# Two model blocks in one kernel: score banks claimed pair by pair, Fourier pieces by halves of the sequence, the first turning and one weight rounding issued earlier

## The reference

```python
for l in range(DEPTH):
    h = _rms_norm(x, norm_g[l])
    p = h @ w_in[l]
    c_q, c_kv, k_pe, z_a, u_f, z_f, g_a, g_f = _split_in(p)
    o_a = _mla_branch(c_q, c_kv, k_pe, ...)                # 8 heads, 96 = 64 + 32 (rotated) dimensions
    y_a = (o_a * jax.nn.silu(z_a)) @ w_attn_proj[l]
    y_f = (_fourier_branch(u_f) * jax.nn.silu(z_f)) @ w_fourier_proj[l]
    m = (jax.nn.sigmoid(g_a + b_merge[l, 0]) * y_a
         + jax.nn.sigmoid(g_f + b_merge[l, 1]) * y_f)
    x = x + m @ w_out[l]
```

## Time and profile before

| what | value |
|---|---|
| time, median of 3 runs | 2191.68 us (2191.34 to 2194.15) |
| profiled execution, its time | 2191.92 us |
| profiled execution, its span | 2190.1 us |
| granted TensorE clock, mean | 0.995 of full speed |
| busy: TensorE, VectorE, ScalarE, GpSimd | 97%, 43%, 42%, 35% of the span |
| instructions | 29154 |

### The profile page before, as it was taken

How to read it: one execution, slowest core, us unless ns; L and a number is a source line. 1 busy time by engine, 2 the same in 40 slices (tenths; PEclk the granted TensorE clock), 3 DMA queues, 4 the chain that set the end, 5 groups by cost and what they waited for, 6 DMA issues and landing times.

```text
span 2190.1 us, 29154 instructions
## 1 busy us (share of the span) xinstructions
PE 2126.9 (97%) x11190; PEld 1660.1 (76%) x11190; DVE 949.3 (43%) x1470; ACT 927.8 (42%) x1442; POOL 759.4 (35%) x316
## 2 busy tenths in 40 slices
PE   6999999999999998999999999999899999989999
PEld 5677778888888885667888888777578887856887
DVE  7674462111126267775211112654633354454331
ACT  5642264233245324774422324554643244555231
POOL 3332134444443630003444444334034443401443
PEclk9999999999999999999999999999999999999999
DMA  4232122232332420002333233222013332201332
GB/s 150 68 100 77 53 80 93 91 100 93 96 97 91 134 83 20 1 1 81 97 97 96 96 97 97 77 87 86 1 58 96 97 96 87 78 20 39 97 97 87
DMA packets 60166, 174.84 MB, mean 80 GB/s; under 512 B 17040, under 2 KB 17168, under 8 KB 60048
## 3 DMA queue, kind: packets, MB, share of 16 engines
q1 hardware_dynamic: 47456, 168.38, 24.4%
q10 hardware_dynamic: 12592, 4.75, 0.9%
HBM read 169.44 MB, written 3.67 MB: 79 GB/s over the span
## 4 chain that ended last, share of the span: by engine, by line
issue 65%; POOL 21%; PE 12%; ACT 1%; POOLq 1%; DVE 0%; DVEq 0%
POOL w_lo L2549 21%; PE banks L731 4%; PE banks L733 3%; PE banks L732 3%; PE banks L1235 1%; ACT prob L1808 1%; ACT probT L1815 0%; PE banks L1247 0%; PE banks L1239 0%; ACT prob_far L1808 0%; POOLq L2553 0%; POOLq L2555 0%; PE banks L1213 0%; PE banks L1291 0%; POOLq L2549 0%
## 5 line engine op out<-in xcount | busy, mean ns | idle before, releaser
L2549 POOL TENSOR_TENSOR w_lo<-raw,w_hi 128x1024 fp32r<-128x1024 f32 x312 | 759.2, 2435 | 1414.5 <-ACT w_hi L1375 1414.4
L731 PE MATMUL banks<-h_lo,w_hi 128*128 128x512 f32 x1408 | 570.5, 405 | 23.1 <-DVE h_lo L1910 12.2
L733 PE MATMUL banks<-h_hi,w_hi 128*128 128x512 f32 x1408 | 554.3, 394 | 0.0
L732 PE MATMUL banks<-h_hi,w_lo 128*128 128x512 f32 x1408 | 550.3, 391 | 0.0
L1375 ACT ACTIVATE w_hi<-raw 128x1024 fp32r<-128x1024 f32 x312 | 328.1, 1053 | 509.0 <-PE banks L733 497.6
L731 PEld LDWEIGHTS banks<-h_lo,w_hi 128*128 128x128 f32 x1408 | 266.1, 189 | 89.0 <-POOL w_lo L2549 16.4
L732 PEld LDWEIGHTS banks<-h_hi,w_lo 128*128 128x128 f32 x1408 | 265.9, 189 | 60.6 <-issue 4.4
L733 PEld LDWEIGHTS banks<-h_hi,w_hi 128*128 128x128 f32 x1408 | 265.7, 189 | 60.8
L731 PE MATMUL banks<-a_lo,w_hi 128*128 128x512 f32 x768 | 304.3, 396 | 0.0
L733 PE MATMUL banks<-a_hi,w_hi 128*128 128x512 f32 x768 | 301.5, 393 | 0.0
L732 PE MATMUL banks<-a_hi,w_lo 128*128 128x512 f32 x768 | 298.7, 389 | 0.0
(11 more groups left out here) (360 smaller groups left out, 2513.7 us busy)
## 6 DMA issues: line engine op xcount, KB each, us to landing
raw<-in_weights SPq DMA_DIRECT2D x312, 512.0 KB, 3.5
x<-in_x SPq DMA_DIRECT2D x4, 512.0 KB, 6.7
out<-x SPq DMA_DIRECT2D x8, 256.0 KB, 2.0
phase<-in_phase ACTq DMA_DIRECT2D x1, 706.0 KB, 4.1
phase<-in_phase ACTq DMA_DIRECT2D x1, 704.0 KB, 4.0
ld_dram<-Ld ACTq DMA_DIRECT2D x1, 512.0 KB, 5.0
Ls<-ld_dram ACTq DMA_DIRECT2D x1, 512.0 KB, 4.8
inv_dram<-inv ACTq DMA_DIRECT2D x1, 512.0 KB, 2.8
```

The source lines that it names most:

```text
L731: mm(out, w_hi, x_lo, start=first, stop=False)
L732: mm(out, w_lo, x_hi, start=False, stop=False)
L733: return mm(out, w_hi, x_hi, start=False, stop=last)
L2549: return nc.gpsimd.tensor_tensor(c.w_lo[:, slot, :], c.raw[:, slot, :], c.w_hi[:, slot, :].bitcast(F32), ALU.subtract)
```

## The change

It has four parts, all in the second block, and each is made in both layers.

1. `scores` claims the bank pair of its first item, issues that item's two 64-row matmuls, and then claims the second pair.
2. The transposes of item 0 are issued before the scores of quad 1, and no longer behind them.
3. The Fourier pieces are made half by half (`k` outside, `g` inside) on all engines. The Fourier products wait only for the pieces of their own half, go group by group within a half, and the first three groups announce themselves singly.
4. ScalarE rounds the block two beyond that of the values before the exponentials of the key roots, by `passed("v2", l, 0)`.

```diff
@@ -462,10 +462,10 @@
         for n in range(len(MLA_ITEMS)):
             take_pair(("s2", l, n), (2, 4)[n % 2])
             take_pair(("t2", l, n), 6)
-        for g in range(FG):
-            for k in range(FK):
+        for k in range(FK):
+            for g in range(FG):
                 scratch("dd", l, g, k)
-        gemm([("f", l, g) for g in range(FG)], FK)
+        gemm([("f", l, g) for g in range(FG)], FK, apart=True)
         splits(*[("of", l, g) for g in range(FG)])
         for m in range(KT):
             each("ga", l, m, n=1)
@@ -1229,8 +1229,9 @@
         def scores(quad):
             jj, qt = quad // NT, quad % NT
             t, keys = slice(qt * P, qt * P + P), [("s2", l, 2 * quad + i) for i in range(2)]
-            outs = [claim_pair(key) for key in keys]
+            outs = []
             for i in range(2):
+                outs.append(claim_pair(keys[i]))
                 for s in range(2):
                     mm(outs[i][:, s, :], c.q2[pair[s], 4 + 2 * jj + i, t], c.k2[pair[s], 2 * jj + i, :], start=True, stop=False)
             for i in range(2):
@@ -1271,10 +1272,11 @@
             gemm((("za", "zf")[z // 4], l, z % 4), h_hi, h_lo)
             if z in (1, 2):
                 query_sums(2 * z, 2 * z + 2)
+        turned_probs(0)
         for q in range(1, MLA_QUADS + 2):
             if q < MLA_QUADS:
                 scores(q)
-            if q <= MLA_QUADS:
+            if 1 < q <= MLA_QUADS:
                 turned_probs(2 * q - 2)
             if q > 1:
                 values(2 * q - 3)
@@ -1296,17 +1298,17 @@
                 ins.then_inc(fill(key), 1)
         outs = [claim(("f", l, g)) for g in range(FG)]
         first = block[("f", l, 0)][0]
-        for g in range(FG):
-            for k in range(FK):
-                read(("dd", l, g, k))
         for k in range(FK):
             pe.wait_ge(c.w_lo_ready, first + k + 1)
-            for part in range(2):
-                w, d = slice(part * T, part * T + T), slice(part * P, part * P + P)
-                for g in range(FG):
-                    slot = (first + k) % RING
+            slot, last = (first + k) % RING, k == FK - 1
+            for g in range(FG):
+                read(("dd", l, g, k))
+                for part in range(2):
+                    w, d = slice(part * T, part * T + T), slice(part * P, part * P + P)
                     ins = three(outs[g][:, :], c.d_hi[:, k, g, d], c.d_lo[:, k, g, d], c.w_hi[:, slot, w], c.w_lo[:, slot, w],
-                                k == part == 0, k == FK - 1 and part == 1)
+                                k == part == 0, last and part == 1)
+                if last and g < FG - 1:
+                    ins.then_inc(fill(("f", l, g)), 1)
             ins.then_inc(c.block_used, 1)
         for m in range(KT):
             gemm(("ga", l, m, 0), h_hi, h_lo)
@@ -1779,6 +1781,7 @@
 
         value_out(0)
         value_out(1)
+        passed("v2", l, 0)
         for i in range(4):
             read(("hs2", l, "k", i))
             f(c.k_root[:, i, :], c.k_root[:, i, :], ACT.Exp, scale=-0.5).then_inc(c.k_root_ready, 1)
```

## The result

The changed kernel takes 2181.16 us (median of 5 runs, 2179.26 to 2182.59); the kernel before took 2191.75 beside it. The ratio is 0.9945, 95% interval 0.993 to 0.9959. The forecast was 2174.8 us, in a range of 2170.5 to 2179: it had the direction and missed the size. Of 16.9 us forecast, 10.6 came.

What follows compares the result with a forecast made beforehand. TensorE was taken as the bound, so gains lay in its waits. Per layer 5.1 - 0.56 + 1.2 + 1.1 + 1.6 = 8.44 us, 16.9 for two, gave 2174.8 us; range 2170.5 to 2179.

Steps and rivals of the forecast that it cites:

- the end of the Fourier products: Before the first merge gate: signalling groups singly removes TensorE's 0.88 us wait and the slow start, 1.1 us saved a layer.
- some later stage gives the time back: Listed sign of being wrong: time saved is lost again later in the kernel; given no size or chance.
- The split claim: Attention's quad loop: half the first pair's scores run inside the wait; 0.85 us saved a quad, 5.1 us a layer.
- the 7.5 that I had named as a sign of being wrong: Quad loop: period forecast at about 7.6 us; above 8 or under 7.5 us would show the forecast wrong.
- the row that I went by: Second pair's weight load: starts only at the wait's end, giving 0.85 us a quad; loading ahead would give 0.93.
- the 0.26 us from ScalarE's read to the scores: Quad loop: delay from ScalarE's last read of a bank pair to scores, used to place the first pair's claim at 1546.06.
- The price of 0.08 us for the late start: Scores' second half: passes beginning after a wait are slower at first, about 0.08 us added to its 0.98 us.
- The first turning: Item 0's transposes ahead of the second quad's scores: exponentials and the next claim come later, 0.56 us lost a layer.
- The rounding: Second attention gate's weight block rounded before the key roots: TensorE's 1.41 us wait and slow start go, 1.6 us saved.
- The pieces: Fourier pieces made half by half: first product starts behind the last piece without its 1.13 us wait, 1.2 us saved.
- that rival: A Fourier wait comes back, from late banks or GpSimd's roundings: 2.3 us of a layer lost, 2179.4 us; chance 8%.
- The loop's last wait: Before the last quad's transposes: the 1.84 us wait stays, since it hangs on ScalarE's four exponentials.

## Why the prediction missed

**The step that failed** is the one on the end of the Fourier products: "The wait of 0.88 goes, and with it the slow start [...] I take 1.1 us, bounds 0.88 and 1.15." The wait and the slow start did go (1.0 us). What was left out is that the wait also separated two rows of matmuls with different paces. Without it the 767 matmuls behind keep the Fourier products' 233.3 ns, 4.4 ns more than their own, which is 3.3 us of a layer and 6.6 us in all. The term should have been +2.3, not -1.1. Had it stood so, the forecast would have been 2181.6 us. That this lies so near the measured 2181.16 is luck: the waits gave 3.1 us more than forecast in the two layers, and the scatter ahead of the changed part took 2.7. No rival priced it. The list of what would make the forecast wrong had "some later stage gives the time back", but with no mechanism and no weight. The row that could have warned me was in the trace of before: its Fourier products took 12.31 - 1.0 = 11.3 us for 48, or 233 to 235 ns each, beside 228.9 in the gates, projections and output products. (The value products, which also have the operands exchanged, run at 233 too.)

**The split claim** was mis-sized: forecast 0.85 us of a quad, measured (5.99 + 0.38) / 6 = 1.06. I had the new period at 7.6 us with ScalarE's chain ending last. It is 1554.05 - 1546.67 = 7.38, under the 7.5 that I had named as a sign of being wrong. TensorE about three quads of the changed kernel, from the third:

```profile
1538.77 1.13 PE L1236 MATMUL banks<-k,q 64*128 64x512 f32 x4 [1.12 <-ACT prob_far L1811]
1540.29 1.13 PE L1236 MATMUL banks<-k,q 64*128 64x512 f32 x4 [0.39 <-ACT prob L1811]
...
1546.67 2.12 PE L1236 MATMUL banks<-k,q 64*128 64x512 f32 x8
1548.72 1.14 PE L1240 MATMUL banks<-k_pe,q 32*128 32x512 f32 x8
1549.80 1.09 PE L1248 MATMUL banks<-common,prob 128*128 128x128 f32 x8
...
1554.05 2.12 PE L1236 MATMUL banks<-k,q 64*128 64x512 f32 x8
```

None of the scores' rows from the fourth quad on has a wait, but these rows merge both halves. ScalarE's last exponential and its read there, and the weight load of the second pair:

```profile
1554.11 0.79 ACT L1811 ACTIVATE prob<-banks,nb,q_root 128x512 f32<-128x512 f32 x1
...
1554.77 0.21 ACT L1811 ACTIVATION_READ_ACCUMULATOR prob<-banks,nb,q_root 128x1 f32 x1
```

```profile
1555.04 0.30 PEld L1236 LDWEIGHTS banks<-k,q 64*128 64x128 f32 x4 [0.69 <-ACT prob L1811]
```

ScalarE's read ends at 1554.98 and the load starts 0.06 us later. By the nanosecond stamps it is 0.05 us in every quad from the third to the last. In the first two quads, whose scores wait for nothing, the second half starts 0.96 us behind the first; from the fourth on it is 0.99. So ScalarE's chain still ends last, as forecast, but by 0.03 us alone. From T to the next second claim it is 1555.04 - 1549.80 = 5.24 us, where I kept 5.46, and the other 2.14 are the 2.13 of the forecast. The term that was wrong is the 0.26 us from ScalarE's read to the scores, which I took from the joint claim of before. That the joint claim's several semaphore checks, one behind the other, made up the 0.2 fits the stamps but was not tried by itself.

On the loads the row that I went by holds: the scores' part takes 2.12 us split and 1.99 whole, and the second pair's load begins with its claim's release. The Trainium skill (TensorE: Matmul & The Clock Gate, Architectural detail) has TensorE's queue pulling loads ahead of matmuls in flight; across this claim the trace shows none pulled ahead. The price of 0.08 us for the late start was about right: 0.13, of which 0.03 is the wait.

**The first turning**: right in sign, and 0.38 us for the forecast 0.56 with the split claim, 0.6 without it. **The rounding**: 1.6 forecast, 1.6 measured, and undoing it gives 1.6 back. **The pieces**: 1.2 forecast, 1.4 measured; no new wait stands before pieces five to eight, so that rival did not come. **The loop's last wait** of 1.8 us stayed, as forecast. The waits alone brought 10.0 us of a layer, 1.6 more than forecast; the pace took 3.3 back, and 2.6 us of scatter ahead of the changed part did the rest.

## What to carry to other kernels

A wait between two rows of matmuls can do work: before removing one, read the distance from matmul to matmul on either side of it, and if they differ, ask which of the two will go on. When TensorE is busy for longer after a change that only removed waits, count matmuls in equal windows at the same granted clock. A short matmul at the seam costs 0.06 to 0.14 us and won back 3.3 us of a layer here.

## What the runs showed of the hardware

- A row of 128x128 by 128x512 float32r matmuls at a granted clock of 1.00 has two steady paces with the same instructions: 228.9 ns in the mean (steps of 226, 229, 232) and 233.3 (steps of 233, 233, 234). The second was carried over from products with the roles of the operands exchanged, whose own pace is 233.3, for 767 matmuls and 179 us. 24 ordinary products at 787 us of the kernel before had it with no such products ahead.
- Those products have two rhythms at the same mean, even (233, 234) and in turns (231, 236). Only the even one was carried on. Two executions of the same code within one kernel took different ones behind pauses of 1.24 and 1.27 us, and so did the two layers of the kernel before behind pauses of 1.13; a short float32r matmul at the start gave the turns in both of the layers in which it was tried.
- From the end of ScalarE's read to TensorE's load or matmul behind it: 0.05 us where one pair of banks was claimed, 0.26 to the matmul where two pairs were claimed together.
- Why the even rhythm is kept, and what chooses between the two at the start, stays open: no run here looks inside the loading of weights.
